# Rotary half exchange issued from GpSimd's queue, RG-LRU's gain and root placed just ahead of its scan, in a two-layer hybrid decoder

## The chip, the cores and the metric

The kernel runs on one core of a Trainium2 chip. The metric is the time of one execution on the device in microseconds (us), as the median of several runs. A core has TensorE (PE: matmuls, into PSUM), VectorE (DVE), ScalarE (ACT), GpSimd (POOL) and SyncE (SP), each with its own instruction stream in order. They meet through semaphores only. DMAs are issued from the queues of SP, ACT and POOL.

## The reference

Two layers, each run over 256 prompt tokens and 8 x 4 sample tokens (T = 288 token columns in all, D = 1024). A layer has a mixing block and a feed-forward block (dense in layer 0, 8 experts in layer 1), each followed by a layer norm. The mixing block projects the stream once and gives it to four groups of heads:

```
xa, ga, qb, kb, vb, ob, ib, fb, qc, kc, vc, gc, qd, fd, id_, gd = split(x @ w_in)
# RG-LRU
a = exp(log_a);  u = sqrt(-expm1(2*log_a)) * (ig * xc);  h = scan(a, u);  ya = h * gelu(ga)
# mLSTM (qb kb vb, gates ib fb, output gate ob), HGRN2 (qd fd id_, output gate gd)
# retention
q = rotary(qc); k = rotary(kc) * DK_C**-0.5
#   rotary: concat([x1*cos - x2*sin, x1*sin + x2*cos]), x1 and x2 the halves of a head
out = concat([ya, yb, yc, yd]) @ w_out
```

## The kernel before, in words

All of it is fp32. Channels lie on the 128 partitions and tokens on the free axis: a group's 256 channels are two tiles of 128 x 288, two heads of 64 to a tile. The projection has 14 panels of two tiles, in the order `FD QD KB QB XA VB KC QC ID VC GA GD GC OB`. Six are plain products (`proj_tile`, `tile_piece`) that ScalarE evicts with `tile(i)`. Eight (`SEVEN`, q = 0 to 7) are done with seven half-size products each: VectorE adds up the weights (`panel_sums`, lines 2652 to 2660), TensorE multiplies in three groups (`seven`), ScalarE evicts each group (`seven(q, g)`), and VectorE adds the results (`first_outputs` at 2667 and 2668, `last_outputs` at 2673 to 2676). The panels KC and QC are q = 2 and 3.

The order on each engine is written out by hand. The function `mix(l)` of each engine lists its steps for layer l, and `need(name, step)` waits for a step of another stream. Between the projection's products TensorE does those of the four groups, so that the other engines have time to prepare them. What the change touches:

- **Rotary embedding.** The sine part needs each head's halves exchanged, which crosses partitions, so it is done by DMA: for each of KC and QC four transfers of 32 partitions x 2 tiles x 288 (72 KB) from `proj` into `rotmp`. `rotmp` shares its memory with the mLSTM's weights `WT`, so it may be written only after the mLSTM's products (`ml_ps` `out`). The issues stand in ScalarE's stream behind `seven(3, 2)` and RG-LRU's root (line 2038), ahead of `tile(16)`. VectorE's `rotate` (lines 2474 to 2476, first KC, then QC) waits for the landing; TensorE's retention scores wait for `rot_q`, behind panel 4's first three products.
- **HGRN2's end decays.** ScalarE computes exponentials behind `tile(16)` (`hg_ac` `ends`); VectorE multiplies them with queries and keys (lines 2759, 2760) just ahead of `rotate`.
- **RG-LRU.** `lru_decay` (line 2434) forms (tanh + 1) * xc in place; `lru_gain` (lines 2438, 2439) forms om from a and h; ScalarE takes the root of om; `lru_scan` (line 2443 on) multiplies, scans and writes the group's output (`lru_dv` `out`), some 40 us after the first two. GpSimd waits for that before its products `values(VM_HG, 2)` and `values(VM_RET, 1)` (line 696), whose results are read by the sample states' products.
- **mLSTM's head norm.** `mlstm_spread` (line 2530) on VectorE, a root on ScalarE (SD_ML), a reciprocal on VectorE (line 2514), then the product with `RR_ML` on TensorE.

Of the kernel before, what the change touches and what calls it, by code (L numbers as in the profile page):

```python
# [17 lines left out]
ACT = mybir.ActivationFunctionType  # L18
AX_X = mybir.AxisListType.X

P = 128
# [4 lines left out]
DEPTH, GW, NH, HD = 2, 256, 4, 64  # L26
# [4 lines left out]
XA, GA, QB, KB, VB, OB, QC, KC, VC, GC, QD, FD, ID, GD = range(0, NPT, 2)  # L31
# [5 lines left out]
WC = WP - 3  # L37
# [182 lines left out]
def decoder_kernel(nc, A, out, tab, where):  # L220
    with ExitStack() as ctx:
# [4 lines left out]
        S = {n: ctx.enter_context(nc.semaphore(n)) for n in SEMAPHORES}  # L226

        def mark(name, step, l):
            return S[name], len(STEPS[name]) * l + STEPS[name].index(step) + 1
# [25 lines left out]
        def ev(tile, l):  # L255
            panel = ORDER.index(tile - tile % 2)
            if panel in SEVEN:
                return seven_out(l, SEVEN.index(panel), 1)
            return S["in_ev"], N_IN * l + dense(2 * panel + tile % 2) + 1
# [65 lines left out]
        proj = cut(OV, 0, NPT, T)  # L325
# [91 lines left out]
        xpad, xc_, r_, ig_, a_, h_, om_ = (cut(scr, 630 * i, 2, WP) for i in range(7))  # L417
        rotmp = cut(MB, 6924, 2, T), cut(MB, 6924 + 576, 2, T)
# [30 lines left out]
        block = ctx.enter_context(nc.Block())  # L449
# [206 lines left out]
        def _(pool):  # L656
# [17 lines left out]
            for l in range(DEPTH):  # L674
                if l:
                    pool.wait_ge(S["lru_ps"], l)
                else:
                    pool.wait_ge(S["tables_in"], 16)
                pool.dma_start(LW[:, :, :, :], A["lru_w"][l].rearrange("p (r a n) -> p r a n", r=2, a=2)).then_inc(S["lru_in"], 16)
                if l:  # L680
                    pool.wait_ge(S["states_stored"], 16 * STORES * l)
                else:
                    pool.wait_ge(full[1], loaded["in", 0, 3])
                for kind in range(3):
                    pool.dma_start(S0[:, kind], A["states"][l, kind]).then_inc(S["s0_in"], 16)
                if l:
                    pool.wait_ge(S["out_ps"], 1)
                    for n in range(2):
                        for i in range(4):
                            weight_sum(n, i)  # L690
                if l:
                    pool.wait_ge(*mark("gate_dv", "gsb", l))
                pool.memset(ATALL, 0.0).then_inc(S["levels_zeroed"], 1)

                def values(vm, kind):
                    pool.tensor_tensor(
                        vm.rearrange("p (b v) -> p b v", b=NB), SAMPLE_VALUES[kind].unsqueeze(1).to_broadcast([P, NB, HD]),
                        tb("batchmask").unsqueeze(2).to_broadcast([P, NB, HD]), ALU.mult).then_inc(S["vm_ready"], 1)

                pool.wait_ge(*mark("ml_ac", "vt", l))  # L700
                values(VM_ML, 0)
                if l == 0:
                    for e in range(NE):
                        pool.dma_start(XG[CAP * e:CAP * e + CAP, :], tab[0:CAP, 0:D]).then_inc(S["xg_zeroed"], 16)
                pool.wait_ge(*mark("lru_dv", "out", l))
                pool.wait_ge(*mark("hg_ac", "vt", l))
                values(VM_HG, 2)
                pool.wait_ge(*mark("ret_ac", "vt", l))
                pool.wait_ge(*mark("ml_dv", "rr", l))
                values(VM_RET, 1)  # L710

                def store(dst, src, **kw):
                    pool.dma_start(dst, src, **kw).then_inc(S["states_stored"], 16)

                def store_states(kind):
                    store(out["prompt_states"][l, kind], PFIN[:, kind].rearrange("p a v -> p (a v)"))
                    store(out["sample_states"][l, kind], S0[:, kind])

                pool.wait_ge(*mark("ml_dv", "states", l))
                store_states(0)  # L720
                store(out["mlstm_m"][l], M1[0:P:HR, :])
                pool.wait_ge(*mark("hg_dv", "states", l))
                store_states(2)
                pool.wait_ge(*mark("lru_dv", "out", l))
                store(out["columns"][l], OUTC[:, 0:90])
                pool.wait_ge(*mark("ret_dv", "states", l))
                store_states(1)
# [1153 lines left out]
        def _(act):  # L1881
            def f(o, i, fn, **kw):
                return act.activation(o, i, fn, **kw)  # L1883
# [38 lines left out]
            def mix(l):  # L1922
                def need(name, step):
                    act.wait_ge(*mark(name, step, l))

                def end(ins, name, step):
                    done(ins, name, step, l)
# [30 lines left out]
                def values(bank, kind, name):  # L1958
                    need(name.replace("_ac", "_ps"), "vt")
                    at, step = VALUES_AT[kind]  # L1960
                    dst = VT[:, 0:2, at:at + NH * step].rearrange("p t (h v) -> p t h v", v=step)[:, :, :, 0:HD]
                    f(dst, PS[:, bank, :].rearrange("p (t h v) -> p t h v", t=2, h=NH), ACT.Copy)
                    end(f(SAMPLE_VALUES[kind], PS[:, bank + 1, 256:256 + HD], ACT.Copy), name, "vt")
# [54 lines left out]
                end(last, "lru_ac", "tanh")  # L2018
                level(6)
                seven(3, 0)  # L2020
                need("lru_dv", "decay")
                need("lru_ac", "tanh")
                for dst, fn in ((a_, ACT.Exp), (h_, ACT.Tanh)):
                    for p in range(2):
# [4 lines left out]
                need("ml_ps", "out")  # L2029
                end(f(Y_ML, PS[:, 4:6, 0:T], ACT.Copy), "ml_ac", "y")  # L2030
                seven(3, 2)
                need("lru_dv", "om")
                end(f(om_[:, :, 0:WC], om_[:, :, 0:WC], ACT.Sqrt, scale=-0.25), "lru_ac", "sqrt")
                for i, (tile_at, landed) in enumerate(((KC, S["swap_k_in"]), (QC, S["swap_q_in"]))):
                    act.wait_ge(*ev(tile_at + 1, l))
                    for block in range(0, P, HD // 2):
                        other = block ^ HD // 2
                        act.dma_start(rotmp[i][block:block + HD // 2], proj[other:other + HD // 2, tile_at:tile_at + 2]  # L2038
                                      ).then_inc(landed, 16)
                tile(16)  # L2040
                need("hg_dv", "ends")
                need("hg_dv", "l6")
# [15 lines left out]
                seven(5, 0)  # L2058
                need("ml_dv", "vs")
                end(f(SD_ML, SD_ML, ACT.Sqrt, bias=VAR_FLOOR), "ml_ac", "sd")  # L2060
                values(2, 1, "ret_ac")
                seven(5, 1)
                seven(5, 2)
# [161 lines left out]
        def _(v):  # L2225
# [134 lines left out]
            def mix(l):  # L2360
                def need(name, step):
                    v.wait_ge(*mark(name, step, l))

                def end(ins, name, step):
                    done(ins, name, step, l)
# [66 lines left out]
                def lru_decay():  # L2432
                    need("lru_ac", "tanh")
                    end(stt(ig, ig, 1.0, xc_[:, :, 0:WC], AD, M), "lru_dv", "decay")

                def lru_gain():
                    need("lru_ac", "decay")
                    link(tt(om, a, a, M))
                    end(stt(om, om, 1.0, hh, AD, M), "lru_dv", "om")
# [53 lines left out]
                def keys(bank, buf, name):  # L2493
                    need(name.replace("_dv", "_ps"), "keys")
                    for t in range(2):
                        dst = KTK[:, buf, t, :].rearrange("p (h d) -> p h d", h=NH)
                        src = PS[:, bank, t * 256:t * 256 + 256].rearrange("p (h d) -> p h d", h=NH)
                        if name == "ret_dv":
                            tt(dst, src, tb("retkeyw")[:, t].unsqueeze(2).to_broadcast([P, NH, HD]), M)
                        else:  # L2500
                            stt(dst, src, HD ** -0.5, mcol[:, t, 1].unsqueeze(2).to_broadcast([P, NH, HD]), M, M)
                    if name == "ret_dv":
                        last = ts(SAMPLE_KEYS[buf], PS[:, bank + 1, 0:HD], tb("retkeys"), None, M)
                    else:
                        last = ts(SAMPLE_KEYS[buf], PS[:, bank + 1, 0:HD], HD ** -0.5, mcol[:, 2, 1, 0:1], M, M)
                    end(last, name, "keys")
# [21 lines left out]
                def mlstm_spread():  # L2528
                    need("ml_ps", "var")
                    end(stt(SD_ML, rlf, HEAD_EPS, PS[:, 6, 0:T], M, AD), "ml_dv", "vs")  # L2530
# [213 lines left out]
                    decay_const()  # L2744
                panel_outputs(2)
                panel_sums(3)
                lru_decay()
                chunk_ends()
                lru_gain()
                merge(5, 2)  # L2750
                operands(6)
                mlstm_outputs()
# [15 lines left out]
                weights(6, 1, "ret_dv", "w23")  # L2768
                panel_sums(5)
                keys(2, 1, "ret_dv")  # L2770
                mlstm_spread()
                panel_outputs(4)
                need("hg_ps", "c0")
# [596 lines left out]
```

## Time and profile before

| | |
|---|---|
| median of 3 runs | 979.9 us (979.84 to 980.01) |
| the profiled execution: its own time | 980.52 us |
| its span, first to last instruction | 978.6 us |
| granted TensorE clock, mean | 0.995 |
| mixing stage of layer 0 | about 0 to 154 us of the span |
| mixing stage of layer 1 | about 424 to 572 us of the span |

The rest of the span is the output projection, the feed-forward block and the norms of each layer, and the experts. All times in the rows are counted from the span's start and come from this one execution. In a timeline a row has the start, the duration, the engine, the line, the operation, its tiles and how many instructions are merged; the bracket at its end is the idle time of the engine ahead of it and who ended it. A matmul's end is modelled.

### The profile page before, as it was taken

To read this page: it belongs to the slowest core of one execution; us is meant where nothing else is said; L and a number is where in the kernel's file an instruction comes from. 1 tells how busy PE (TensorE), PEld (TensorE's weight loads), DVE (VectorE), ACT (ScalarE), POOL (GpSimd) and SP (SyncE) were. 2 spreads that over 40 slices of the span, in tenths; PEclk is the share of its full clock that TensorE was granted. 3 is DMA by queue.
4 is the path that set the end of the run, shared out by engine and by line. 5 is a ranking of instruction groups with operands and counts; after the bars stand their busy time and mean duration, and the time that the engine had idled before them with its cause. 6 is when DMAs were issued, how large, how long until landed. Compare 5 with 4: busy or idle time off the path is not lost.

```text
span 978.6 us, 24212 instructions
## 1 busy us (share of the span) xinstructions
PE 962.9 (98%) x10924; PEld 755.0 (77%) x10924; DVE 488.6 (50%) x999; ACT 195.2 (20%) x414; POOL 82.4 (8%) x105
## 2 busy tenths in 40 slices
PE   9999999999999999999999999999999999999995
PEld 6797887999999999997988888555565656556542
DVE  5897983755566654269879866320101201010125
ACT  1434351221111100044343423300000000000001
POOL 1110033400000000000000200410000020000020
PEclk9999999999999999999999999999999999999998
DMA  9437258224453155201242499799999999999973
GB/s 363 153 103 268 101 183 345 83 87 173 172 205 133 46 204 218 107 17 71 87 154 92 167 373 384 304 345 400 401 422 395 422 391 417 423 423 422 423 279 114
DMA packets 37500, 241.46 MB, mean 247 GB/s; under 512 B 5008, under 2 KB 8144, under 8 KB 17680
## 3 DMA queue, kind: packets, MB, share of 16 engines
q1 hardware_dynamic: 27280, 216.69, 55.7%
q0 software_dynamic: 6432, 19.43, 5.6%
q10 hardware_dynamic: 3680, 3.74, 1.2%
q8 instruction: 88, 1.44, 0.6%
q14 instruction: 20, 0.16, 0.0%
HBM read 228.60 MB, written 13.07 MB: 247 GB/s over the span
## 4 chain that ended last, share of the span: by engine, by line
PE 92%; DVE 5%; ACT 2%; issue 1%; ACTq 0%; DVEq 0%
PE ps L778 70%; PE ps L1426 15%; PE ps L1534 6%; PE ps L781 1%; PE ps L1363 1%; ACT overlay L1883 1%; DVE overlay L2561 0%; ACTq L2038 0%; ACT x L1883 0%; ACT up_slots L1883 0%; ACT L1883 0%; DVE tables L3133 0%; DVE x L2329 0%; DVE overlay L2324 0%; DVE up_slots L2587 0%
## 5 line engine op out<-in xcount | busy, mean ns | idle before, releaser
L778 PE MATMUL ps<-up_slots,mix_or_moe 128*32 128x352 f32 (+2 forms) x3248 | 237.0, 451 | 0.1
L778 PEld LDWEIGHTS ps<-up_slots,mix_or_moe 128*32 128x32 f32 (+2 forms) x3248 | 123.1, 111 | 108.0 <-issue 9.3
L778 PE MATMUL ps<-x,up_slots 128*128 128x144 f32 (+3 forms) x832 | 151.9, 336 | 0.0
L778 PEld LDWEIGHTS ps<-x,up_slots 128*128 128x128 f32 x832 | 125.2, 190 | 23.4 <-issue 7.1
L778 PE MATMUL ps<-overlay,tables 128*32 128x256 f32 (+2 forms) x1952 | 114.5, 377 | 0.3 <-DVE overlay L2318 0.3
L778 PEld LDWEIGHTS ps<-overlay,tables 128*32 128x32 f32 (+2 forms) x1952 | 78.8, 112 | 32.0 <-issue 0.8
L3172 DVE TENSOR_TENSOR mix_or_moe<-mix_or_moe,ps 128x352 f32<-128x352 f32 x24 | 11.2, 516 | 179.1 <-PE ps L778 179.1
L1426 PE MATMUL ps<-overlay,up_slots 128*128 128x144 f32 x704 | 91.7, 286 | 0.6 <-DVE overlay L2948 0.3
L1426 PEld LDWEIGHTS ps<-overlay,up_slots 128*128 128x128 f32 x704 | 88.3, 190 | 1.1 <-issue 0.8
L778 PE MATMUL ps<-up_slots 128*128 128x144 f32 (+2 forms) x960 | 79.5, 257 | 0.5 <-DVE up_slots L2594 0.5
L778 PE MATMUL ps<-overlay,up_slots 128*128 128x128 f32 (+3 forms) x528 | 78.2, 308 | 0.0
L778 PEld LDWEIGHTS ps<-up_slots 128*128 128x128 f32 (+1 forms) x960 | 73.2, 163 | 4.8 <-issue 1.6
L778 PEld LDWEIGHTS ps<-overlay,up_slots 128*128 128x128 f32 x528 | 72.2, 191 | 5.1
L1426 PE MATMUL ps<-x,up_slots 128*128 128x144 f32 x528 | 70.1, 286 | 0.5 <-ACT x L1883 0.5
L1426 PEld LDWEIGHTS ps<-x,up_slots 128*128 128x128 f32 x528 | 66.9, 190 | 0.6 <-issue 0.6
L3162 DVE STREAM_TRANSPOSE tables<-mix_or_moe 128x352 f32<-128x352 f32 x24 | 18.3, 806 | 77.3 <-PE ps L778 77.2
L1883 ACT ACTIVATE up_slots<-ps 128x288 f32<-128x288 f32 (+1 forms) x70 | 30.4, 436 | 110.7 <-PE ps L778 65.8
L1883 ACT ACTIVATE mix_or_moe<-ps 128x352 f32<-128x352 f32 (+5 forms) x44 | 16.7, 437 | 164.5 <-PE ps L778 164.5
L1883 ACT ACTIVATE tables<-ps 128x256 f32<-128x256 f32 (+2 forms) x27 | 9.7, 428 | 178.1 <-PE ps L778 177.7
L1883 ACT ACTIVATE overlay<-ps 128x288 f32<-128x288 f32 (+4 forms) x49 | 19.1, 391 | 94.7 <-PE ps L778 65.6
L1883 ACT ACT_TABLE_LOAD x29 | 37.2, 1283 | 2.1 <-ACT tables L1883 0.9
L1534 PE MATMUL ps<-overlay,up_slots 128*128 128x144 f32 x240 | 30.9, 286 | 0.0
(375 smaller groups left out, 956.8 us busy)
## 6 DMA issues: line engine op xcount, KB each, us to landing
up_slots<-in_moe_w SPq DMA_DIRECT2D x64, 1408.0 KB, 20.5
overlay<-in_moe_w SPq DMA_DIRECT2D x21, 1536.0 KB, 23.4
up_slots<-in_ffn_w SPq DMA_DIRECT2D x30, 1024.0 KB, 6.9
up_slots<-in_w_in SPq DMA_DIRECT2D x27, 1024.0 KB, 5.5
up_slots<-in_w_out SPq DMA_DIRECT2D x8, 1024.0 KB, 7.1
overlay<-in_moe_w SPq DMA_DIRECT2D x7, 1024.0 KB, 23.3
mix_or_moe<-in_states POOLq DMA_DIRECT2D x6, 512.0 KB, 5.0
expert_tokens<-in_shape_tables POOLq DMA_DIRECT2D x8, 384.0 KB, 8.3
```

What stands on the lines that cost most here:

```text
L778: return pe.matmul(o, lhsT, rhs, start=start, stop=stop)
L781: return pe.transpose(o, src, ident[0:k, 0:k])
L1363: last = pe.matmul(PS[:, bank, 0:TH], w[:, k], x[:, k], start=opens and k == 0, stop=k == KH - 1, skip_group_check=not opens)
L1426: last = pe.matmul(PS[:, bank, 0:TH], w[:, k], x(k), start=opens and k == 0, stop=k == KH - 1, skip_group_check=not opens)
L1534: last = pe.matmul(PS[:, bank, 0:TH], w[:, k], x(k), start=opens and k == 0, stop=k == KD - 1, skip_group_check=not opens)
L1883: return act.activation(o, i, fn, **kw)
L3162: v.transpose(HT[:, g], HID[e % 2][:, g].rearrange("p (q i) -> p i q", i=FT)).then_inc(S["ht_done"], 1)
L3172: tt(h, h, PS[:, (3 if e == NE - 1 else 3 * ((e + 1) % 2)) + g, 0:CH], M).then_inc(S["moe_h"], 1)
```

## The change

The eight transfers of the half exchange are issued from GpSimd's queue, behind its wait for the mLSTM's products and ahead of its wait for RG-LRU's output. ScalarE no longer issues them. RG-LRU's root moves on ScalarE from behind `seven(3, 2)` to behind the root of the mLSTM's deviation, and ScalarE's exponential and tanh of the decay no longer wait for `lru_decay`. On VectorE `lru_decay` and `lru_gain` move from around `chunk_ends` to between retention's `keys` and `mlstm_spread`. The arithmetic is the same.

```diff
@@ GpSimd, in the loop over layers
+                pool.wait_ge(*mark("ml_ps", "out", l))
+                for i, (tile_at, landed) in enumerate(((KC, S["swap_k_in"]), (QC, S["swap_q_in"]))):
+                    pool.wait_ge(*ev(tile_at + 1, l))
+                    for block in range(0, P, HD // 2):
+                        other = block ^ HD // 2
+                        pool.dma_start(rotmp[i][block:block + HD // 2], proj[other:other + HD // 2, tile_at:tile_at + 2]
+                                       ).then_inc(landed, 16)
                 pool.wait_ge(*mark("lru_dv", "out", l))
@@ ScalarE, mix
                 seven(3, 0)
-                need("lru_dv", "decay")
                 need("lru_ac", "tanh")
...
                 seven(3, 2)
-                need("lru_dv", "om")
-                end(f(om_[:, :, 0:WC], om_[:, :, 0:WC], ACT.Sqrt, scale=-0.25), "lru_ac", "sqrt")
-                for i, (tile_at, landed) in enumerate(((KC, S["swap_k_in"]), (QC, S["swap_q_in"]))):
-                    act.wait_ge(*ev(tile_at + 1, l))
-                    for block in range(0, P, HD // 2):
-                        other = block ^ HD // 2
-                        act.dma_start(rotmp[i][block:block + HD // 2], proj[other:other + HD // 2, tile_at:tile_at + 2]
-                                      ).then_inc(landed, 16)
                 tile(16)
...
                 end(f(SD_ML, SD_ML, ACT.Sqrt, bias=VAR_FLOOR), "ml_ac", "sd")
+                need("lru_dv", "om")
+                end(f(om_[:, :, 0:WC], om_[:, :, 0:WC], ACT.Sqrt, scale=-0.25), "lru_ac", "sqrt")
                 values(2, 1, "ret_ac")
@@ VectorE, mix
                 panel_sums(3)
-                lru_decay()
                 chunk_ends()
-                lru_gain()
                 merge(5, 2)
...
                 keys(2, 1, "ret_dv")
+                lru_decay()
+                lru_gain()
                 mlstm_spread()
                 panel_outputs(4)
```

## Rows read from the trace of the kernel before

**Rows 1.** The page, part 1: busy us (share of span) xinstructions.

```profile
PE 962.9 (98%) x10924; PEld 755.0 (77%) x10924; DVE 488.6 (50%) x999; ACT 195.2 (20%) x414; POOL 82.4 (8%) x105
```

**Rows 2.** The waits of TensorE: us in total, times, longest.

```profile
PE ps L778 <- DVE overlay L2476: 0.4, 1, 0.4
```

**Rows 3.** Timelines of TensorE, layers 0 and 1: the retention scores.

```profile
103.11 2.04 PE L778 MATMUL ps<-overlay 64*128 64x256 f32 x24 [0.43 <-DVE overlay L2476]
...
519.92 2.04 PE L778 MATMUL ps<-overlay 64*128 64x256 f32 x24
```

**Rows 4.** Timeline of VectorE, layer 0: end-decay product, second rotation's first and last.

```profile
97.15 0.76 DVE L2759 TENSOR_TENSOR up_slots<-up_slots,overlay 128x576 f32<-128x576 f32 x1 [1.67 <-ACT end_decay L1883]
...
100.83 0.76 DVE L2474 TENSOR_TENSOR mix_or_moe<-mix_or_moe,tables 128x576 f32<-128x576 f32 x1
...
102.30 0.76 DVE L2476 TENSOR_TENSOR overlay<-overlay,mix_or_moe 128x576 f32<-128x576 f32 x1
```

**Rows 5.** Timelines around tile 16: its second piece, its eviction, table loads; last, layer 1.

```profile
90.74 2.69 PE L778 MATMUL ps<-x,up_slots 128*128 128x288 f32 x10
...
93.92 0.41 ACT L1883 ACTIVATE overlay<-ps 128x288 f32<-128x288 f32 x1 [4.86 <-PE ps L778]
94.35 1.28 ACT L1883 ACT_TABLE_LOAD   x1
...
511.16 1.28 ACT L1883 ACT_TABLE_LOAD   x1
```

**Rows 6.** Gate of QC (VectorE), then lines 713 (GpSimd), 704 (GpSimd), 2038 (ScalarE): landings.

```profile
89.93 0.45 DVE L2676 TENSOR_TENSOR overlay<-up_slots 128x288 f32<-128x288 f32 x1
...
L713 POOL DMA_DIRECT2D out_prompt_states<-prompt_states x6: 542/577/627, 123.4 to 556.5; - x6
...
DMA to landing us min/median/max: 1.9/3.0/4.1
...
DMA to landing us min/median/max: 3.6/8.3/11.1
...
DMA to landing us min/median/max: 4.0/5.4/6.2
```

**Rows 7.** Timeline of VectorE, layer 1: `lru_decay` and the second of `lru_gain`.

```profile
494.75 0.80 DVE L2434 SCALAR_TENSOR_TENSOR up_slots<-up_slots 128x624 f32<-128x624 f32 x1
...
498.72 0.81 DVE L2439 SCALAR_TENSOR_TENSOR up_slots<-up_slots 128x624 f32<-128x624 f32 x1
```

**Rows 8.** Timelines of all engines, layer 1: RG-LRU's root, then from retention's keys on.

```profile
505.60 0.72 ACT L1883 ACTIVATE up_slots<-up_slots 128x624 f32<-128x624 f32 x1
...
527.60 0.74 DVE L2499 TENSOR_TENSOR mix_or_moe<-ps,tables 128x256 f32<-128x256 f32 x2
...
527.15 0.27 PE L778 MATMUL ps<-tables,overlay 64*32 64x64 f32 x5
...
529.03 0.30 DVE L2668 TENSOR_TENSOR up_slots<-up_slots 128x144 f32<-128x144 f32 x1
...
530.09 0.41 ACT L1883 ACTIVATE up_slots<-ps 128x288 f32<-128x288 f32 x1 [2.00 <-PE ps L778]
...
531.81 0.44 ACT L1883 ACTIVATE overlay<-overlay 128x288 f32<-128x288 f32 x1
...
532.36 1.95 DVE L2514 RECIPROCAL overlay<-overlay 128x288 f32<-128x288 f32 x1 [0.53 <-ACT overlay L1883]
...
536.53 1.34 PE L778 MATMUL ps<-overlay,mix_or_moe 128*64 128x128 f32 x24
...
538.25 2.05 POOL L696 TENSOR_TENSOR up_slots<-mix_or_moe,tables 128x512 f32<-128x512 f32 x2 [50.36 <-DVE out_cols L2456]
...
539.42 1.42 DVE L2652 TENSOR_TENSOR up_slots<-up_slots 128x512 f32<-128x512 f32 x1
...
541.64 2.12 PE L778 MATMUL ps<-up_slots 128*128 128x144 f32 x16
...
551.39 1.28 DVE L2794 TENSOR_TENSOR mix_or_moe<-mix_or_moe,ps 128x512 f32<-128x512 f32 x2 [2.26 <-PE ps L778]
```

## The prediction

> **What bounds the kernel now.** I read the totals first [rows 1]: TensorE is busy for 962.9 us of a span of 978.6, 98%, VectorE for half and ScalarE for a fifth of it. So an edit to work of VectorE, ScalarE or GpSimd is worth only the idle time of TensorE that it takes away, and the list of what TensorE waited for comes next. In both mixing stages together, with all that the change touches, it holds one entry: 0.4 us behind line 2476 [rows 2]. The timelines give the place [rows 3]. In layer 0 TensorE starts the retention scores at 103.11 after 0.43 of waiting for the second rotation; it was free at 102.68. In layer 1 the same scores start at 519.92 with no idle time. The gap is in one layer alone; all that the change can bring in these stages is 0.43, unless the profile hides something.
>
> What makes the rotation late is read backwards on the other engines. The second rotation ends at 103.06; it starts at 100.83 and runs for 2.23, and VectorE has not stood idle since it began the products with the end decays at 97.15; before those it stood idle for 1.67, for ScalarE's end decays [rows 4]. ScalarE evicted projection tile 16 at 93.92, though TensorE had it ready at 90.74 + 2.69 = 93.43, because its queue was issuing the exchanges until then; then it loaded a table for 1.28 before the exponentials [rows 5]. The ones that hold the issuing queue are the exchanges of the queries: their source is complete only when VectorE ends line 2676 at 90.38 [rows 6].
>
> **Part 1, the square root leaves its place.** It sat between tanh/exp and exp, so it cost a table load before it and one behind it. Behind SD's root it shares that one's table. Two loads of 1.28 go per layer. Only the second stood on the way to the rotation: in layer 1 it starts at 511.16, and the exponentials with it now start 1.28 earlier [rows 5].
>
> **Part 2, the exchange leaves ScalarE's queue.** Eight issues per layer go. In layer 0 tile 16 is then evicted at 93.47 and not at 93.92, 0.45 earlier; in layer 1 the eviction already followed its product. Together VectorE's products with the end decays can start 1.73 earlier in layer 0 and 1.28 in layer 1. Merge 7 ahead of them waits for TensorE; in layer 0 it ends at 95.5, 1.67 ahead of 97.15, so 1.67 is what is left. The first rotation moves by as much, the second from 100.83 to 99.16, and ends at 101.4. TensorE wants it at 102.68: the gap of 0.43 goes, with 1.3 to spare. In layer 1 nothing goes; the spare time grows by 1.28.
>
> **Part 3, the exchange enters GpSimd's queue.** Nothing waits behind it there: the next thing is the value product for HGRN2, which waits for the scan some 30 us later (the end of the scan). The keys' four transfers start at the end of the mLSTM products, about 4 us ahead of now, and cannot matter. The queries' four start at 90.4 in layer 0. An issue costs 0.54 to 0.63 on this queue [rows 6], so the last starts at 90.4 + 3 x 0.58 = 92.15. (In layer 1 everything is 417.2 later for this gate: the last starts at 509.4.) The trace of before shows no exchange on this queue, so its landing is bounded: from below by the 1.9 of the small state stores, from above by the 11.1 of the 384 KB transfers that queued behind each other; the nearest rows are the exchange itself from ScalarE, 4.0/5.4/6.2, and GpSimd's stores, 1.9/3.0/4.1 [rows 6]. I take 6: landed at 98.2 and 515.4, 1 us ahead of the new start of the rotation in both layers. The rotation may start as late as 102.68 - 2.28 = 100.4 (517.6 in layer 1) before TensorE notices, so the deadline is a landing of 8.2. At 11.1 it would start at 103.25 and 520.5, and the scores at 105.5 and 522.8: 2.4 and 2.9 later than now. The same bound on the low side gains nothing, because the gap is only 0.43.
>
> What the row shows on GpSimd's issues beside VectorE: the stores from 123.4 on ran while VectorE had an instruction after the other, and still took 0.54 to 0.63 each [rows 6]. The Trainium skill, "SBUF — State Buffer", section "Who interferes with whom" and the box on "The DVE blocks DMA trap", says the opposite can happen: GpSimd's descriptors need the port that a two-port VectorE instruction holds, about 3.1 us where 0.62 are normal, and it advises ScalarE's or SP's queue instead, which is this change turned round. By its figure (an estimate) four issues would take 12.4 and the scores would slip by some 5 us per layer.
>
> **Part 4, RG-LRU's gain on VectorE.** Three instructions move from ahead of merge 5 to behind the retention keys: the first takes 0.80, of which 0.08 lies beside its successor, and the other two 0.81 each with 0.03 between them (one of them is shown) [rows 7]: 0.72 + 0.81 + 0.03 + 0.81 = 2.37. Where they were, VectorE had idle time in front of merge 5, so their going brings nothing there in layer 1. Where they come to they cost all of it. In layer 1: VectorE is 1.28 ahead, so it reaches the keys at 526.3, but TensorE has transposed them only at 527.15 + 0.27 = 527.42; they start there, 0.15 ahead of 527.60, and the three push everything behind them by 2.2. Now follow who needs it [rows 8]. The first outputs of panel 4 end at 529.03 + 0.30 = 529.33 now and at 531.5 then; ScalarE's eviction for panel 5, at 530.09 now, waits for them, takes its 0.41, and the table load follows at 531.9. With 1.28 for the table and 0.44 for the root the deviation ends at 533.7, so the reciprocal starts at 533.8, 1.4 later than 532.36; that is less than 2.2, since it waited for 0.53. RG-LRU's root of 0.72 follows the deviation at once and ends by 534.4, ahead of the scan. The chunk state c1 behind the reciprocal ends at 536.0 (534.6 now); TensorE wants it at 536.53. **Spare: 0.5.** The scan and its end are 1.4 later too, so GpSimd's two products start at 539.65 and end at 541.7. The first sum of panel 6 takes 1.42 now and ends at 540.84, 0.54 behind those products, as if it waited for them; then it ends at 542.25. TensorE needs it for the fourth product of panel 6, half way through the sixteen matmuls that start at 541.64, at 542.67. **Spare: 0.4.** Later there are 2.26 of idle VectorE before the HGRN2 states, which swallow the 1.4. In layer 0 TensorE comes 0.43 earlier to all of this, its keys too, and the spare times come out the same. I cost part 4 at 0; it is hidden behind TensorE's own work, and if a spare time is overrun the excess goes to the span, once per layer.
>
> **The sum.** Layer 0: -0.43; layer 1: 0. Everything behind layer 0's mixing is released by TensorE's progress, the weights' loads too, so the 0.43 reaches the end. The profiled execution took 980.52 (span 978.6 and 1.9 around it) and would take 980.1; the median of the runs is 979.9, 0.6 below that execution, and goes to 979.5.
>
> **The rivals.**
> - *A spare time of part 4 is overrun.* For it: 0.4 and 0.5 are the sums of five or six steps, and the wait behind GpSimd's products is of a kind that jumps. Against it: the steps are long rows seen in both layers. If each layer overruns by 0.5, it is -0.43 + 1.0: 980.5.
> - *The queries' exchange lands late on GpSimd's queue* (the other side). The place is the second rotation, and it decides from a landing of 8.2 behind the last issue. For it: the 11.1 and a median of 8.3 on this very queue; in their case 3 MB stood in line, and the exchange has 72 KB apiece. At 11.1 it is +2.4 + 2.9: 985.2. The starved descriptors above end in the same place.
> - *The gap stays.* The rotation is not what TensorE waits for, or another wait takes its place at 102.7 (the values of HGRN2, the mLSTM's centring, which stand before it on other engines): 979.9. The trace shows none that would be late.
> - *A gain beyond TensorE's idle time,* over 2 us, for instance because matmuls that the profile models as busy were waiting. The two layers run the same matmuls in these stages in the same time but for the gap, which speaks against it: 977.5.
>
> **How the numbers follow.** Forecast (979.3 to 979.8) 0.66; spare time overrun (979.8 to 980.9) 0.14; gap stays 0.08; late exchange 0.07; larger gain 0.05. The time is the likeliest's, 979.5. The range of 978.9 to 980.9 holds the first three. 0.2% is 2 us, about what a measurement tells from no change; the first three lie within it, 0.88; faster 0.05, slower 0.07.
>
> **What would show it.** Right: four fewer table loads (25); the idle 0.43 ahead of the retention scores of layer 0 gone; VectorE's second rotation of layer 0 starting near 99.2; GpSimd issuing two groups of four in each layer; the reciprocal of the mLSTM 1.4 later in layer 1. Wrong: idle time of TensorE ahead of the scores (late exchange), ahead of the HGRN2 outputs at 536.5, or within panel 6 at 542.7 (spare times); or VectorE waiting for a DMA at line 2474.

## The result, and the profile after

| | median us | lowest to highest | runs |
|---|---|---|---|
| before | 980.42 | 979.33 to 980.95 | 17 |
| after | 982.20 | 981.21 to 983.83 | 17 |

The ratio is 1.0019, 95% interval 1.0013 to 1.0026: slower by 0.19%, some 1.8 us. The forecast was 979.5 with a range of 978.9 to 980.9; it was a gain of 0.43 counted from a median of 979.9 of three runs, which is 0.5 below the 980.42 here. The profiled execution of the changed kernel took 982.33 (span 980.4; before 980.52 and 978.6).

The waits of TensorE in the changed kernel (us in total, times, longest; compare [rows 2]):

```profile
PE ps L788 <- DVE overlay L2676: 2.6, 2, 1.3
```

The entry behind the rotation is gone. In its place stand two waits of 1.3, one per layer, behind VectorE's line 2676, the last step of a panel's outputs. (TensorE's helper lines moved down by 7: 778 is 785, 781 is 788.) The timeline of TensorE in the changed kernel, first layer 0, then layer 1 from the scores on ([rows 3] has the scores before):

```profile
102.15 0.60 PE L788 MATMUL ps<-tables,overlay 128*128 128x128 f32 x4
102.68 1.77 PE L785 MATMUL ps<-overlay 64*128 64x256 f32 x24
104.28 0.29 PE L785 MATMUL ps<-tables,overlay 64*32 64x64 f32 x8
...
115.43 0.63 PE L788 MATMUL ps<-tables,overlay 128*128 128x128 f32 x4 [1.28 <-DVE overlay L2676]
...
520.03 0.60 PE L788 MATMUL ps<-tables,overlay 128*128 128x128 f32 x4
520.56 1.77 PE L785 MATMUL ps<-overlay 64*128 64x256 f32 x24
522.16 0.30 PE L785 MATMUL ps<-tables,overlay 64*32 64x64 f32 x8
...
533.30 0.63 PE L788 MATMUL ps<-tables,overlay 128*128 128x128 f32 x4 [1.28 <-DVE overlay L2676]
```

What waits are four transposes of `overlay`, where the projection lies: `values(A_, VC)`. VC is panel 4 of the seven-product panels, so it waits for `panel_outputs(4)`. VectorE in the changed kernel, layer 1 (the three RG-LRU instructions, then those outputs; compare [rows 7, 8]):

```profile
526.35 0.69 DVE L2660 TENSOR_TENSOR up_slots<-up_slots 128x512 f32<-128x512 f32 x1
527.87 0.76 DVE L2499 TENSOR_TENSOR mix_or_moe<-ps,tables 128x256 f32<-128x256 f32 x2 [0.83 <-PE ps L785]
528.54 0.28 DVE L2503 TENSOR_SCALAR mix_or_moe<-ps,tables 128x64 f32<-128x64 f32 x1
528.73 0.80 DVE L2434 SCALAR_TENSOR_TENSOR up_slots<-up_slots 128x624 f32<-128x624 f32 x1
529.45 0.80 DVE L2438 TENSOR_TENSOR up_slots<-up_slots 128x624 f32<-128x624 f32 x1
530.28 0.81 DVE L2439 SCALAR_TENSOR_TENSOR up_slots<-up_slots 128x624 f32<-128x624 f32 x1
531.01 0.44 DVE L2530 SCALAR_TENSOR_TENSOR overlay<-overlay,ps 128x288 f32<-128x288 f32 x1
...
532.71 0.45 DVE L2676 TENSOR_TENSOR overlay<-up_slots 128x288 f32<-128x288 f32 x1
```

Before, VectorE's output of layer 1 was done ahead of TensorE's transposes. The rows are that output, then the transposes ahead of the scores and those of VC, in layer 1 and, last, in layer 0:

```profile
530.15 0.45 DVE L2676 TENSOR_TENSOR overlay<-up_slots 128x288 f32<-128x288 f32 x1
...
519.34 0.60 PE L781 MATMUL ps<-tables,overlay 128*128 128x128 f32 x4
...
531.58 0.66 PE L781 MATMUL ps<-tables,overlay 128*128 128x128 f32 x4
...
102.08 0.60 PE L781 MATMUL ps<-tables,overlay 128*128 128x128 f32 x4
...
114.77 0.66 PE L781 MATMUL ps<-tables,overlay 128*128 128x128 f32 x4
```

VectorE was done at 530.60, and TensorE came at 531.58, 0.98 later. In the changed kernel the transposes start 0.14 behind the end that releases them (533.16, then 533.30), so 0.84 of it was spare. The retention keys, from which VectorE works on to these outputs, start 0.27 later than before (527.87 against 527.60), while TensorE itself is 0.38 later there (527.53 against 527.15); that makes 0.95. The three instructions push the next step by 2.28 (528.73 to 531.01), since the third overlaps its successor too; the prediction had 2.37. 2.28 less 0.95 is 1.33: the wait is the inserted work less what was spare.

**Where 1.8 us come from.** From the last transposes ahead of the scores to the transposes of VC, layer 0 takes 13.28 (102.15 to 115.43) and layer 1 13.27 (520.03 to 533.30). Before, layer 1 took 531.58 - 519.34 = 12.24, and layer 0 114.77 - 102.08 = 12.69, with its gap of 0.43. So +0.59 and +1.03, 1.62 together. The experiments below that have neither the new wait nor the late rotation (1, 3 and 7) take 11.92 to 11.93 in both layers. Against these the new wait costs 1.35 to 1.36 per layer, a little more than the 1.28 of the bracket, and the earlier rotation is worth 0.77 in layer 0 and 0.32 in layer 1. The remaining 0.2 of the two spans' difference lies elsewhere, 0.07 of it ahead of layer 0's scores.

**A wait that the matmul view hides.** The gain is larger than the gap. Before, the scores' stretch took 1.86 in layer 1 (519.92 to 521.78) without any idle time shown, now 1.60 (520.56 to 522.16). A matmul's end is modelled and lies past the start of the next, which covers short waits. The view of weight loads doesn't. TensorE's weight loads before, layer 1, first half of the scores and second half, and last the first half in the changed kernel:

```profile
519.92 0.19 PEld L778 LDWEIGHTS ps<-overlay 64*128 64x128 f32 x2 [0.22 <-DVE overlay L2476]
...
520.84 0.19 PEld L778 LDWEIGHTS ps<-overlay 64*128 64x128 f32 x2 [0.19 <-DVE overlay L2510]
...
520.56 0.19 PEld L785 LDWEIGHTS ps<-overlay 64*128 64x128 f32 x2 [0.17 <-issue]
```

The second half waits for line 2510, the centring of the mLSTM's output, which VectorE does right behind the rotation and ended at 520.79. It was late in both layers, with the same 0.19 at 104.03 in layer 0; the earlier rotation brings it forward too. Not all of a bracket in this view is waiting: the first half has 0.17 of "issue" even where the rotation is early. But with 0.22 and a rotation that ended at 519.87, 0.05 ahead of 519.92, the rotation of layer 1 had no spare time before; the scores start 0.58 behind the transposes there and 0.53 in the changed kernel. So layer 1 gains 0.26 at the centring and some 0.05 at the rotation.

### The profile page after: what moved, and what is told of

Its sections match the earlier page's. It is cut to its first block, busy times and chain, and to the rows that moved or that the text cites. A ratio compares the mean times of both kernels' runs of the same rounds, so it can differ in the third digit from the quotient of the medians.

```text
span 980.4 us, 24208 instructions
## 1 busy us (share of the span) xinstructions
PE 962.2 (98%) x10924; PEld 754.7 (77%) x10924; DVE 488.6 (50%) x999; ACT 189.2 (19%) x410; POOL 90.0 (9%) x121
## 4 chain that ended last, share of the span: by engine, by line
PE 92%; DVE 5%; ACT 1%; issue 1%; DVEq 0%; ACTq 0%
PE ps L785 70%; PE ps L1433 15%; PE ps L1541 6%; PE ps L788 1%; PE ps L1370 1%; ACT overlay L1890 1%; DVE overlay L2561 0%; ACT x L1890 0%; DVE tables L3133 0%; DVE x L2329 0%; DVE x L2311 0%; DVE overlay L2324 0%; DVE overlay L2317 0%; DVE up_slots L2587 0%; DVE mix_or_moe L2499 0%
```

## The experiments

The theory: the exchange's and the root's moves gain about 0.95; VectorE's three RG-LRU instructions hold back panel 4's outputs and cost 1.28 per layer. Rivals: GpSimd's queue costs the time; the late root on ScalarE does; the late reciprocal, c1 or scan does. Each comparison is with runs of the kernel before on the same chip; its medians were 980.28 for the first four and 980.35 for the rest.

**1. The three instructions back in their old place**

```diff
                 panel_sums(3)
+                lru_decay()
                 chunk_ends()
+                lru_gain()
...
-                lru_decay()
-                lru_gain()
                 mlstm_spread()
```

> The changed kernel, but lru_decay and lru_gain stand on VectorE where they stood before; the exchange stays on GpSimd's queue and the root stays late. Theory (the three RG-LRU instructions hold back VectorE's outputs of panel 4, and TensorE's transposes of VC wait for them, 1.28 per layer; the exchange itself gains): both waits of 1.28 go, the scores' gap of 0.43 and about 0.26 of slower scores per layer stay gone. Expected -0.9 to -1.0 against the kernel before. Rival (GpSimd's queue, its descriptors or their DMAs cost the time): still +1.8. Rival (the late root on ScalarE costs it): still +1.8.

Measured: 979.28, ratio 0.9989 (0.9980 to 0.9998), 1.0 us faster than before. TensorE in this kernel, layer 0, has no idle time ahead of the transposes, 11.92 behind those ahead of the scores:

```profile
101.34 0.60 PE L788 MATMUL ps<-tables,overlay 128*128 128x128 f32 x4
...
112.64 0.69 PE L785 MATMUL ps<-mix_or_moe 128*64 128x64 f32 x16
113.26 0.66 PE L788 MATMUL ps<-tables,overlay 128*128 128x128 f32 x4
```

GpSimd's queue and the late root are both still there, so neither costs the time.

**2. The exchange back on ScalarE's queue, all else as changed**

```diff
-                pool.wait_ge(*mark("ml_ps", "out", l))
-                (the two loops of pool.dma_start)
...
                 seven(3, 2)
+                (the two loops of act.dma_start)
                 tile(16)
```

> The changed kernel, but the exchange is issued from ScalarE again, ahead of tile 16; RG-LRU's instructions and root stay late. Theory: the two waits of 1.28 stay, so +1.4 to +1.9; since the table load goes with the root, the rotation is still 1.3 earlier and the scores' gap is gone here too. Rival (GpSimd's queue costs the time): the loss goes, -0.5 to 0. Rival (the exchange's move alone brought the rotation forward): the 0.43 is back, and the time is above the changed kernel's by 0.4 to 0.9.

Measured: 982.02, ratio 1.0018 (1.0009 to 1.0027), the changed kernel's own time. Its waits of TensorE (the helpers' lines are here those of before, VectorE's one less):

```profile
PE ps L781 <- DVE overlay L2675: 2.6, 2, 1.3
```

and its scores, layer 0:

```profile
102.00 0.60 PE L781 MATMUL ps<-tables,overlay 128*128 128x128 f32 x4
102.53 1.77 PE L778 MATMUL ps<-overlay 64*128 64x256 f32 x24
```

The loss stays without GpSimd's exchange, and the gap stays away without it, since the root is still late. 1.7 above the kernel before is as expected (+1.4 to +1.9).

**3. The same three instructions, still late, one place further on**

```diff
                 keys(2, 1, "ret_dv")
-                lru_decay()
-                lru_gain()
                 mlstm_spread()
                 panel_outputs(4)
+                lru_decay()
+                lru_gain()
```

> The changed kernel, but lru_decay and lru_gain stand behind panel_outputs(4) and not ahead of mlstm_spread: the same work, still late, just behind what TensorE waits for. Theory: waits of 1.28 gone, -0.9 to -1.0 as e1. Rival (the three instructions cost through the reciprocal, c1 and the scan, whose spare times the prediction gave as 0.5 and 0.4): a wait ahead of the HGRN2 outputs or in panel 6, and a time above e1's by 0.3 to 1.

Measured: 979.45, ratio 0.9988 (0.9979 to 0.9997). The entry behind line 2676 is gone from TensorE's waits and no other has come up in the mixing stages; the stretch is 11.92 in both layers. So it is no matter of "late", but of which side of panel 4's outputs the work is on.

**4. Only `lru_gain` late**

```diff
                 panel_sums(3)
+                lru_decay()
                 chunk_ends()
...
-                lru_decay()
                 lru_gain()
                 mlstm_spread()
```

> The changed kernel, but lru_decay is early again and only lru_gain is late: 1.65 of VectorE in the late place and not 2.37. Theory (the wait is the inserted time less a fixed spare time of about 1.1): 2.37 gives 1.28, so 1.65 gives 0.56 per layer, and the time is +0.1 to +0.3. Rival (a wait that does not scale, such as the root's on ScalarE): 1.28 per layer stays, +1.8.

Measured: 980.63, ratio 1.0006 (0.9997 to 1.0015). TensorE ahead of the transposes of VC, layer 0 and layer 1:

```profile
113.66 0.63 PE L788 MATMUL ps<-tables,overlay 128*128 128x128 f32 x4 [0.57 <-DVE overlay L2676]
...
530.70 0.63 PE L788 MATMUL ps<-tables,overlay 128*128 128x128 f32 x4 [0.57 <-DVE overlay L2676]
```

0.56 was expected. 0.72 less of VectorE is 0.71 less of waiting: past the spare time the cost is one for one. The median is 0.35 above the kernel before, where 0.1 to 0.3 was expected; the interval holds both.

**5. The consumer moved instead of the producer**

```diff
@@ TensorE
-                need("ret_dv", "keys")
-                values(A_, VC)
-                value_rows(A_, VC, "ret_ps")
                 seven(5, 3, 7)
+                need("ret_dv", "keys")
+                values(A_, VC)
+                value_rows(A_, VC, "ret_ps")
@@ ScalarE
-                values(2, 1, "ret_ac")
                 seven(5, 1)
                 seven(5, 2)
+                values(2, 1, "ret_ac")
```

> The changed kernel with RG-LRU's instructions as late as it has them, but TensorE transposes VC behind panel 5's last products and not ahead of them (ScalarE's eviction of these values stands behind panel 5's too): the consumer is moved, not the producer. Theory (the only thing that the three instructions make late is TensorE's wait for panel 4's outputs): the waits of 1.28 go, -0.9 to -1.0 against the kernel before, as e1. Rival (c1 and the first sum of panel 6 are late too, spare 0.5 and 0.4 in the prediction): new waits of up to 0.5 per layer ahead of the HGRN2 outputs or in panel 6, and -0.5 to 0.

Measured: 978.85, ratio 0.9988 (0.9979 to 0.9997). VectorE's order is the changed kernel's, and the loss is gone. The median is 1.5 below the kernel before, where 0.9 to 1.0 was expected (by the ratio 1.2, with 0.3 to 2.1 in its interval). This run also tests the two spare times of the prediction, since TensorE is not held up ahead of them. VectorE's c1, the scan's neighbour sum, and TensorE's HGRN2 outputs and panel 6, layer 0:

```profile
117.36 0.37 DVE L2778 SCALAR_TENSOR_TENSOR prompt_states<-chunk_state,end_decay,ps 128x64 f32<-128x64 f32 x2
...
122.18 0.79 DVE L2652 TENSOR_TENSOR up_slots<-up_slots 128x512 f32<-128x512 f32 x1
```

```profile
117.99 1.34 PE L785 MATMUL ps<-overlay,mix_or_moe 128*64 128x128 f32 x24
...
121.03 1.25 PE L785 MATMUL ps<-x,up_slots 128*128 128x144 f32 x8
```

c1 ends at 117.73, 0.26 ahead of TensorE (0.5 was given); the sum ends at 122.97 and is wanted at about 124.1, three products of 1.03 behind 121.03, so 1.1 is spare there (0.4 was given). Neither is a wait.

**6. The exchange on GpSimd's queue alone**

```diff
                 seven(3, 0)
-                need("lru_dv", "decay")
...
                 seven(3, 2)
                 need("lru_dv", "om")
                 end(f(om_[:, :, 0:WC], om_[:, :, 0:WC], ACT.Sqrt, scale=-0.25), "lru_ac", "sqrt")
-                (the two loops of act.dma_start)
                 tile(16)
@@ GpSimd
+                pool.wait_ge(*mark("ml_ps", "out", l))
+                (the two loops of pool.dma_start)
```

> The kernel before with the exchange on GpSimd's queue as the only change of order. Theory (the rotation is held back by ScalarE's queue only in layer 0 and by 0.45): rotation 0.45 earlier in layer 0, the gap of 0.43 gone there, scores from their start to the next stretch 1.6 to 1.7 in layer 0, but still 1.86 in layer 1; -0.5 to -0.7. Rival (the whole gain is the exchange's): -0.95 and 1.60 in both layers.

Measured: 980.31, ratio 0.9996 (0.9987 to 1.0005), by the measured time no change, where -0.5 to -0.7 was expected; the interval (-1.3 to +0.5) can't tell the two apart. The timelines show more: tile 16 and the table load on ScalarE, the second rotation on VectorE, then TensorE's scores, all of layer 0:

```profile
93.49 0.41 ACT L1890 ACTIVATE overlay<-ps 128x288 f32<-128x288 f32 x1 [4.41 <-PE ps L785]
93.92 1.28 ACT L1890 ACT_TABLE_LOAD   x1
...
100.41 0.76 DVE L2474 TENSOR_TENSOR mix_or_moe<-mix_or_moe,tables 128x576 f32<-128x576 f32 x1
...
102.68 2.04 PE L785 MATMUL ps<-overlay 64*128 64x256 f32 x24
104.54 0.30 PE L785 MATMUL ps<-tables,overlay 64*32 64x64 f32 x8
```

The rotation is 0.42 earlier than in [rows 4] and the gap is just closed, as expected. The stretch of the scores is still 1.86 in layer 0, where 1.6 to 1.7 was expected: that was a miss. TensorE comes to the scores as much earlier as the centring does, so it waits for it as before. From transposes to transposes this kernel takes 12.25 in both layers: 0.44 less than before in layer 0, nothing in layer 1.

**7. The late root alone**

```diff
                 seven(3, 2)
-                need("lru_dv", "om")
-                end(f(om_[:, :, 0:WC], om_[:, :, 0:WC], ACT.Sqrt, scale=-0.25), "lru_ac", "sqrt")
                 (the exchange)
...
                 end(f(SD_ML, SD_ML, ACT.Sqrt, bias=VAR_FLOOR), "ml_ac", "sd")
+                need("lru_dv", "om")
+                end(f(om_[:, :, 0:WC], om_[:, :, 0:WC], ACT.Sqrt, scale=-0.25), "lru_ac", "sqrt")
```

> The kernel before with RG-LRU's root behind the mLSTM's root on ScalarE as the only change; the exchange is issued from ScalarE, RG-LRU's instructions are early. Theory (the table load is what held the rotation in both layers): rotation 1.3 earlier in both, gap gone, scores 1.60 in both layers, -0.9 to -1.0 as e1, without GpSimd's queue. Rival (exchange): 0 to -0.3.

Measured: 979.42, ratio 0.9992 (0.9983 to 1.0001). Its scores, layer 0 and then layer 1:

```profile
101.46 1.77 PE L778 MATMUL ps<-overlay 64*128 64x256 f32 x24
103.06 0.29 PE L778 MATMUL ps<-tables,overlay 64*32 64x64 f32 x8
...
517.92 1.77 PE L778 MATMUL ps<-overlay 64*128 64x256 f32 x24
519.51 0.29 PE L778 MATMUL ps<-tables,overlay 64*32 64x64 f32 x8
```

1.60 and no gap in both layers: the timeline has all that the first experiment has, with one instruction moved and the exchange where it was. From transposes to transposes it is 11.93 and 11.92. The times alone leave it just open: the interval touches no change.

**8. Is it the centring?** The first experiment's kernel, with the centring one place later:

```diff
-                center(6, Y_ML, "ml_dv")
                 panel_sums(4)
+                center(6, Y_ML, "ml_dv")
```

> e1 with one instruction moved: VectorE centres the mLSTM's output behind panel_sums(4) and not ahead of it, some 2.5 later; the rotation stays where it is. It asks whether the second half of the scores waits for that centring, so that it explains why the scores' stretch was 1.86 before in a layer without idle time and is 1.60 in the changed kernel. Theory (yes): the stretch grows by about 1.5 in both layers and the time is +1.8 to +2.2 against the kernel before. Rival (the stretch is longer for the rotation's sake or by TensorE's own pace): 1.60 stays, about -0.9.

Measured: 982.38, ratio 1.0022 (1.0013 to 1.0031), 2.0 slower than before, where the first experiment was 1.0 faster. TensorE, layer 0:

```profile
101.84 0.92 PE L785 MATMUL ps<-overlay 64*128 64x256 f32 x8
104.01 1.12 PE L785 MATMUL ps<-overlay 64*128 64x256 f32 x16 [1.25 <-DVE overlay L2510]
```

The stretch is 3.10 (101.84 to 104.94) and not 1.60, 1.5 more, as expected, and as much in layer 1. The bracket says 1.25: here too the modelled end covers a quarter of a microsecond of the wait.

## Why the prediction was wrong

**The step that failed** is in part 4, "Now follow who needs it". Its list of those who wait behind the three instructions names ScalarE's eviction, the reciprocal, c1, the scan and the sum of panel 6. It leaves out the nearest of all: TensorE's transposes of VC, which wait for the last outputs of panel 4. The trace of before and the prediction's own push of 2.2 would have given it: outputs done at 530.60, pushed to 532.8, wanted at 531.58, so 1.2 late and with 0.14 for the release 1.36 per layer; the runs show 1.35. The prediction followed the first outputs of that panel and who waits for those, but not the last ones, and so put part 4 at 0. No wait in the profile of before pointed to it, because a wait that does not happen leaves no entry; only the `pe.wait_ge(*ev(tile + 1, l))` in the code of `values`, with the panels' order, does. Experiments 1, 3 and 5 show it from the side of the producer and of the consumer, 4 that it scales.

**Part 1 and 2, the rotation.** Right for layer 0 in mechanism and in its times: the second rotation of layer 0 was forecast at 99.16 and starts at 99.12, four table loads are gone (25 left), the gap is gone. Too small in size: 0.43 was taken for all that could go, and "unless the profile hides something" was not followed up. It hid 0.26 per layer of waiting for the centring, and "In layer 1 nothing goes" took a start without idle time in the matmul view for spare time, though the rotation ended 0.05 ahead of it. Worth 0.77 and 0.32, not 0.43 and 0. And nearly all of it is the root's: with the root alone moved the stretch is as short as with both moves (experiment 7), the exchange's move alone gives 0.44 in layer 0 only (experiment 6).

**Part 3, the exchange on GpSimd.** Harmless, as said, and better than the value taken. The changed kernel's line 710:

```profile
L710 POOL DMA_DIRECT2D mix_or_moe<-overlay x16: 496/498/550, 82.9 to 510.4; - x16
...
DMA to landing us min/median/max: 1.9/2.7/5.2
```

An issue takes 0.50 and a landing 2.7, at most 5.2, where 6 was taken; from ScalarE's queue it was 4.0/5.4/6.2 [rows 6]. The late landing did not come, nor did starved descriptors: VectorE went without a break from 90.59 to 93.54 through two-input TENSOR_TENSORs and short copies out of PSUM, and the four issues of layer 0 from 90.74 on still took 0.5 each. This is no test of the box on the "DVE blocks DMA" trap in the Trainium skill, "SBUF — State Buffer", which the prediction drew on: the box speaks of VectorE's 2-port modes, and the section "Who interferes with whom" says that `tensor_tensor` has none. The trace agrees: the prediction's estimate from 3.1 us did not apply to the TENSOR_TENSORs that fill most of this stretch.

**Part 4, the rest.** The pushes were right: the reciprocal of layer 1 started at 534.25; forecast was 533.8, plus the 0.38 by which TensorE came later to the retention keys. The spare times held, though the one of c1 is 0.26 and not 0.5 where it can be seen.

**The rivals.** The one that came true is the first, an overrun of spare time, at another place than those priced and at 1.35 per layer, not 0.5. With the prediction's -0.43 and its base of 979.9 that would have given 982.2, the measured time, but by luck: the base was 0.5 too low and the gain 0.66 too small. Two of the reasons given against other rivals were wrong as well. "The trace shows none that would be late" was said of the mLSTM's centring among others, and it was late in both layers. That matmuls modelled as busy were not waiting was read from the two layers being alike; they were alike since both hid the same wait. The range ended at 980.9 since it was built on the two places that had been looked at.

## What to carry to other kernels

Before work is inserted into an in-order stream, list every consumer of every step behind it, up to the next idle time that swallows the delay, and set each step's end against the time at which its consumer arrives. A wait that is not in the profile can be created, so this list comes from the code and its times from the trace. Past the spare time the cost is one for one. Where a change seems to bring several moves, run each by itself: here one of three was worth nearly the whole gain and another was the whole loss. And a consumer that shows no idle time need not have any to spare: its spare time is its start less its producer's end.

## What the runs showed that was not expected

- Matmul rows hide waits of about a quarter of a microsecond; the rows of the weight loads show them, with who ended them (0.19 behind line 2510 where the matmul view has nothing). The same stretch in a run without the wait gives the size: 1.86 less 1.60.
- The same 72 KB transfers landed sooner from GpSimd's queue (median 2.7; 2.8 and 2.7 in experiments 1 and 6) than from ScalarE's (5.4, also in experiment 7). No run tests why.
- GpSimd's two products were expected to hold back VectorE's sum in panel 6. In the changed kernel they took 2.57 and not 2.05, the first sum 0.69 and only the second 1.42:

```profile
122.27 2.57 POOL L696 TENSOR_TENSOR up_slots<-mix_or_moe,tables 128x512 f32<-128x512 f32 x2 [29.57 <-DVE out_cols L2456]
...
123.24 0.69 DVE L2652 TENSOR_TENSOR up_slots<-up_slots 128x512 f32<-128x512 f32 x1
123.97 1.42 DVE L2655 TENSOR_TENSOR up_slots<-up_slots 128x512 f32<-128x512 f32 x1
```

  GpSimd's second product began at 123.28, just behind VectorE's first sum, and took 1.56 where it otherwise takes 1.04. Before, it began at 539.25, ahead of that sum, which then took 1.42 [rows 8]. So in these rows the one that starts second takes longer, and a wait read in one order can't be carried over to another.
- What stays open: whether the times of experiments 1, 3, 5 and 7 differ. Their medians lie from 978.85 to 979.45, within each other's scatter. By the traces experiment 5 is 0.15 per layer ahead of the others: from the last transposes ahead of the scores to the HGRN2 outputs it takes 16.72 (101.27 to 117.99), they 16.87 or 16.88. All four are below both kernels, experiment 7 with the least change.
